# Which partitions of an expert's tile hold its tokens: a different order of the slots in every quarter

## The reference, cut to what matters

```
g_sel = argmax(t @ w_grp);  top_v, top_i = top_k(softmax(le_g), 2)
hid = einsum('nd,edf->nef', t, w_ein);  a, b = split(hid, 2)
act = silu(a) * b * combine[..., None]
out = einsum('nef,efd->nd', act, w_eout)
```

## Time and profile before

| | us |
|---|---|
| median of 3 runs | 752.68 (752.38 to 754.17) |
| profiled execution, its own time | 754.95 |
| span of the profiled execution | 753.3 |
| TensorE busy in the span | 697.9 (93%) |
| experts' stage, from the first sorted weights in flight to the last result row read | about 505 to 734 |

### The profile page before, as it was taken

One profiled execution on the slowest core, in us unless ns is written; L12 is line 12 of the kernel. 1 busy time (PEld: TensorE's weight loads), 2 busy tenths in 40 slices (PEclk: granted clock), 3 DMA queues, 4 the chain that ended last, 5 costly groups with the idle time before them and its releaser, 6 DMA issues.

```text
span 753.3 us, 12490 instructions
## 1 busy us (share of the span) xinstructions
PE 697.9 (93%) x4624; PEld 387.9 (51%) x4624; DVE 285.4 (38%) x898; ACT 171.9 (23%) x410; POOL 84.4 (11%) x127
## 2 busy tenths in 40 slices
PE   5899999999999999889999999999999997777894
PEld 2656666558765665544566666665333322222332
DVE  1553333621101787765451322484411211111257
ACT  0214444212101554332233001321110101110102
POOL 0301000001500334110000000001212121112000
PEclk9999999999999999999999999999999999999998
DMA  8999996727335883899999993538999999999981
GB/s 242 385 387 436 372 379 223 306 88 276 113 113 222 314 302 112 305 322 392 392 367 387 415 423 141 199 100 296 419 415 420 418 417 419 420 419 418 420 272 72
DMA packets 63269, 236.09 MB, mean 313 GB/s; under 512 B 9732, under 2 KB 20877, under 8 KB 48292
## 3 DMA queue, kind: packets, MB, share of 16 engines
q1 hardware_dynamic: 52884, 218.73, 74.7%
q0 software_dynamic: 6432, 14.74, 5.4%
q10 hardware_dynamic: 3888, 1.77, 0.9%
HBM read 230.52 MB, written 19.14 MB: 331 GB/s over the span
## 4 chain that ended last, share of the span: by engine, by line
PE 69%; SPq 13%; DMA 9%; DVE 3%; issue 3%; ACTq 1%; ACT 1%; POOL 0%; POOLq 0%; DVEq 0%
PE bank L637 14%; SPq L486 7%; PE bank L1189 6%; PE bank L1041 5%; PE bank L1068 5%; SPq L505 4%; DMA arena<-in_w_eout 4%; PE bank L1216 3%; PE bank L687 3%; PE bank L565 3%; PE bank L767 2%; PE bank L991 2%; PE bank L904 2%; DMA arena<-in_cmp_pages 2%; PE bank L866 2%
## 5 line engine op out<-in xcount | busy, mean ns | idle before, releaser
L1189 PE MATMUL bank<-arena 128*32 128x512 f32 (+1 forms) x896 | 107.6, 594 | 15.8 <-DMA arena<-in_w_ein 15.8
L637 PE MATMUL bank<-arena 128*128 128x320 f32 x384 | 106.6, 433 | 1.0 <-DVE arena L1596 1.0
L637 PEld LDWEIGHTS bank<-arena 128*128 128x128 f32 x384 | 71.5, 189 | 35.5 <-issue 6.4
L1189 PEld LDWEIGHTS bank<-arena 128*32 128x32 f32 (+1 forms) x896 | 30.6, 111 | 82.0 <-issue 73.7
L1216 PE MATMUL bank<-arena 128*32 128x512 f32 (+1 forms) x464 | 58.3, 595 | 6.6 <-DMA arena<-in_w_eout 6.2
L2076 DVE COPY arena<-bank 128x512 f32<-128x512 f32 x14 | 9.7, 692 | 105.8 <-PE bank L1147 105.8
L1518 ACT ACTIVATE arena<-bank 128x256 f32<-128x256 f32 x16 | 6.2, 386 | 148.6 <-PE bank L1189 145.3
L1041 PE MATMUL bank<-arena 128*128 128x320 f32 (+2 forms) x144 | 35.6, 408 | 0.0
L1216 PEld LDWEIGHTS bank<-arena 128*32 128x32 f32 (+1 forms) x464 | 15.6, 112 | 38.5 <-issue 30.0
L1342 ACT ACTIVATE arena<-bank 32x320 f32<-32x320 f32 x60 | 25.8, 430 | 41.7 <-PE bank L637 41.1
L1068 PE MATMUL bank<-arena 128*128 128x320 f32 x128 | 35.0, 432 | 0.0
(11 more groups left out here) (416 smaller groups left out, 1028.8 us busy)
## 6 DMA issues: line engine op xcount, KB each, us to landing
arena<-in_w_ein SPq DMA_DIRECT2D x52, 1024.0 KB, 25.4
arena<-in_w_eout SPq DMA_DIRECT2D x26, 1024.0 KB, 26.7
arena<-in_w_ada SPq DMA_DIRECT2D x12, 2048.0 KB, 12.4
arena<-in_w_in SPq DMA_DIRECT2D x10, 2048.0 KB, 9.0
arena<-in_k_pages SPq DMA_DIRECT2D x64, 320.0 KB, 6.3
arena<-in_v_pages SPq DMA_DIRECT2D x64, 320.0 KB, 9.5
arena<-in_w_ein SPq DMA_DIRECT2D x3, 4096.0 KB, 22.4
arena<-in_w_eout SPq DMA_DIRECT2D x3, 2048.0 KB, 16.3
```

Of the source, the lines that this page charges most:

```text
L637: m = mm(banks[c % 4][:, 0:N], ring[q][:, k, P * (c % 4):P * (c % 4 + 1)], hT[:, k, :], start=(k == 0), stop=(k == KD - 1))
L1189: m = mm(banks[2 + p % 2][r:r + n, :], xeT[p % 2][:, k, r:r + n], wi2[p % 3][:, e, k, :], start=(k == 0), stop=(k == KD - 1))
```

## The change

The constants alone change. In every quarter, the last eight partitions (24 to 31) now hold slots 4, 9, 14, 19, 24, 27, 29 and 31; the other 24 slots, in order, go to partitions 0, 8, 16, 1, 9, 17, 2, 10, 18, and so on up to 23. No instruction, DMA, wait or byte count is added or removed; the same number of slots is filled, in other partitions.

```diff
-    c[:, C_PLACE:C_PLACE + P] = (r // 32 * 32 + r % 4 * 8 + r % 32 // 4)[None, :]
+    place = r // 32 * 32 + r % 4 * 8 + r % 32 // 4
+    late = (4, 9, 14, 19, 24, 27, 29, 31)
+    others = [n for n in range(32) if n not in late]
+    for block in (0, 1, 2, 3):
+        for n, slot in enumerate(others):
+            place[32 * block + n % 3 * 8 + n // 3] = 32 * block + slot
+        place[32 * block + 24:32 * block + 32] = [32 * block + slot for slot in late]
+    c[:, C_PLACE:C_PLACE + P] = place[None, :]
```

## The result

The changed kernel takes 756.86 us, median of 7 runs (755.18 to 758.04), beside 753.01 for the kernel before (7 runs, 752.38 to 754.17): ratio 1.0043, 95% interval 1.0027 to 1.006, that is 2.0 to 4.5 us slower, 3.2 by the ratio itself and 3.85 between the two medians. Timed again later, beside parts of the change, it gave 1.0036 (1.0018 to 1.0053). The forecast was 755.9, 3.2 slower.

A forecast was written before the change was run, and what follows sets the result against it. The most loaded DMA engine was taken to end the experts' stage; 26 more rows at 0.146 us give 3.8, instruction packets allow 1.6, so 3.2 us slower, 755.9 us. Range 753.3 to 757.3.

The forecast's parts named there:

- Rival 1: Experts' stage: one engine's lateness doesn't matter, the stream has one rate; same time, 752.7 us; chance 0.09.
- Four neighbours of quarters 0 and 1, or 2 and 3, share an engine: Gathers and scatters: four neighbouring partitions of one quarter share a DMA engine with the same four of the next quarter.
- Rival 4: Experts' stage: eight neighbours share an engine; fullest 90 rows to 89, no change, 752.6 us; chance 0.04.
- The price of a filled slot, 0.146 us: Row queue: moving one token to another engine moves 0.157 - 0.011 = 0.146 us, an empty slot still having a tiny packet.
- rival 3: Row queue: a filled slot costs more, 0.185 or 0.2 us; 4.0 to 5.2 us slower, 756.7 to 757.9; chance 0.07.
- The fullest engine goes from 84 to 110 rows: 26 x 0.146 = 3.8 us: Gathers 3 to 15, scatters 0 to 13: added rows on the fullest engine delay the stage's end by 3.8 us, upper bound.
- The doubt about the instruction packets: Stage's end: instruction packets, 1.1 us each, up to two, may make another engine last before; cost down to 1.6 us.
- The figure of 3.2 us: Whole kernel: loss chosen in the upper half of the bounds 1.6 and 3.8 us, as three of the five fullest engines gain.
- Rival 2: Experts' stage: instruction packets sit on engines that lose rows; +1.6 us or less, 753.3 to 754.3; chance 0.11.
- Rival 5: Experts' stage: slow engines with each half's last partitions set the end and lose 20 rows; 2.9 us faster, 749.8; chance 0.03.
- The signs named for the profile: Next profile: last output weights near 729, DMA share falling earlier and deeper, TensorE's waits about 3 us more, scatter 4 0.3 later.
- The last scatter "0.3 later": Scatter 13 on the ending chain: up to 2 more rows, 0.3 us, covered by the last weights and already in the sum.

The follow-up runs named there:

- e1: The changed layout with the eight groups of four partitions of quarters 1 and 3 turned on by one group; ratio to the kernel before 1.0015 (0.9998 to 1.0031).
- e9: Kernel before with a table of places giving engine 8 alone 110 rows, the other fifteen even loads; ratio to before 1.002 (0.9994 to 1.0045).
- e11: Kernel before with a table of places giving engine 3 110 rows, engines 8 to 15 73 to 74; ratio to before 1.0057 (1.0035 to 1.0079).
- e2: Kernel before with slot n of a quarter in partition n, 136 rows on the fullest engine; ratio to before 1.0084 (1.0066 to 1.0103).
- e6: The change made in quarters 0 and 1 only, quarters 2 and 3 as in the kernel before; ratio to before 1.0028 (1.0006 to 1.005).
- e4: Kernel before with the order of the eight groups of four partitions reversed in all quarters; ratio to before 1.0017 (1.0001 to 1.0033).
- e7: Kernel before with the even table of places, worked out from this input's counts, nearly equal rows within each eight engines; ratio to before 0.9982 (0.9964 to 1.0001).
- e12: The even table of places timed again, unaltered, against the kernel before; ratio 0.9989 (0.9968 to 1.0011).
- e10: Kernel before with a table of places giving engine 8 136 rows, the other fifteen 63 to 65; ratio to before 1.0055 (1.0034 to 1.0077).
- e3: Kernel before with the order of the eight groups of four partitions reversed in quarters 1 and 3; ratio to before 1.0005 (0.9991 to 1.0019).

## Why the prediction was right, and where it was not

- **The stage ends with its most loaded engine, and not with the mean: right.** Same packets, same bytes, same dense stream, and the last landing moves between 193.1 and 200.4 us with the layout alone. Rival 1 falls.
- **Four neighbours of quarters 0 and 1, or 2 and 3, share an engine: right.** e1 differs from the change only in which groups of four meet on an engine. Quarters 0 with 2 would leave it as uneven as the change (109 rows each), and 0 with 3 does not fit e9 to e11. Rival 4 falls. The scatters' landings, from which I took it, are thin evidence: in e2 pairs 3 to 7 have 8 rows each on their fullest engine, and their scatters land after 8.2 to 9.8 us, pair 8 with 7 rows after 8.0.
- **The price of a filled slot, 0.146 us: right,** within a tenth (0.146 by the end of the span, 0.16 by the landing, 0.162 - 0.009 by the packets). The 0.185 and 0.2 of rival 3 are too high.
- **"The fullest engine goes from 84 to 110 rows: 26 x 0.146 = 3.8 us": the sum was right, the engine was not.** Engine 8 had 1.8 us of room and accounts for 2.0 of the 3.8 (e9). Engines 0 to 7 carry the same rows in e6 as in the change, and cost 1.8 there. Of the rest only 10, 12 and 14 gain rows. Engine 12 has 74 rows in the even table, one more than before, and that lands 1.0 earlier, so it had over 1.1 of room and 23 x 0.146 - 1.1 = 2.3 is the most it can cost; engine 14 gains 15 rows, 2.2. That leaves engine 10, with 79 to 104 rows: 25 x 0.146 = 3.65, beside 3.8 and 4.0 measured. So the last engine before was, or was level with, one of those of which the prediction said that it "gains rows too", with 3.4 to 3.7. This is worked out by elimination, and takes it that an engine keeps its room from one layout to the next; no row of a view names an engine.
- **The doubt about the instruction packets: the right size.** The two rooms measured, 1.8 us at 84 rows and 3.3 at 62, mean that apart from rows engine 3 is (84 - 62) x 0.146 - (3.3 - 1.8) = 1.7 us later than engine 8; the prediction allowed two packets of 1.1. That these packets make the rooms is still an argument: no run moved one. So what makes one engine later than another apart from its rows stays open.
- **The figure of 3.2 us: a hit, in part by luck.** It was a compromise between 1.6 and 3.8, made for the doubt about which engine is last. That doubt took nothing off: the last weights came the whole 3.8 later, the upper bound. The end is only 3.1 later because the last scatter, issued 3.5 later, took 0.8 less, where the prediction had up to 0.3 more, and the read took 0.4 more.
- **Rival 2** (the last engine before loses rows, 1.6 or less) falls: the time is 2.0 to 4.5 us longer and the last weights 3.8. **Rival 5** falls with the result, and with e4. The Trainium skill ("DMA: Bandwidth & Descriptors", section "Latency and other measured facts") calls engines 7 and 15 usually slower than the others; with 80 and 84 rows on them (e4) the last weights landed 194.2 us after the first scatter, as before, so this case's traces do not show them behind those that set the end. The Trainium skill's section "The descriptor swizzle" on that page gives this grouping of partitions for a plain transfer of 1 MiB; e1 and e9 to e11 bear it out for the indirect DMAs here.
- **The signs named for the profile.** Last output weights near 729: 728.5. DMA share lower and earlier: 0.72, 0.69, 0.49. Scatter 4 later by 0.3: 0.2, 8.2 against 8.0. TensorE's waits up by 3 us: wrong, they grew by 1.7, from 15.8 + 6.2 to these (us, times, longest):

```profile
PE bank L1189 <- DMA arena<-in_w_ein: 16.6, 11, 3.4
PE bank L1216 <- DMA arena<-in_w_eout: 7.1, 7, 1.6
```

  The other part is in the clock: from 600 to 690 the mean granted clock was 0.98 (1.00 before), so some of the same work took longer, by an estimate 0.02 of 71.69 = 1.4 us, and that much less waiting was left. The two profiles of the even table bear this out: 15.6 + 5.8 us of waits at 1.00 (e7), 14.4 + 5.3 at 0.98 (e12), with last weights 0.2 apart or less. So does e11, whose last weights are 3.7 late at 1.00: 15.9 + 8.8, 2.7 more than before. The weights set the pace either way.
- **The last scatter "0.3 later": wrong.** It took 0.84 less (7.93 against 8.77). While it is in flight the DMA share is 0.74 with the change, both times, and 0.59 in e2, and it takes 7.8 to 7.9 us; in the kernel before and eight others with it on the chain the share is 0.90 to 1.02 and it takes 8.55 to 8.97. In e10 it is not on the chain, and there too the share is 0.68 and it takes 7.84. It seems to land sooner where some engines have already run out of weights, and that outweighs two more rows; no run varied it alone.

## What to carry to other kernels

Where a stream keeps all 16 DMA engines busy and every transfer waits for its slowest engine, count the extra work per engine over the whole stretch: the fullest engine sets the cost, not the mean, and an uneven tile is harmless if the others load other engines (e1). Find first which partitions share an engine; spreading slots over the wrong groups, here eight neighbours instead of four, piles them up. And the engine with the most rows need not be the one that ends last: load one engine alone to measure its room.

## What the runs showed of the hardware that was not expected

- The engines are not alike apart from their rows: with 110 rows on engine 8 the last weights land after 196.2 us, with 110 on engine 3 after 197.9, and with the even table just four engines end 1.3 to 1.8 us behind all others.
- The stage begins at different times from one profile to the next: the first scatter lies between 528.7 (e9) and 533.0 (e3), for which I have no cause. It is not the table's doing as far as the times can tell, for they side mostly with the count from the first scatter and not with the span: e9, e6 and e11 have spans 1.7 and 0.2 shorter and 1.3 longer than before, from the first scatter they are 1.3, 2.2 and 4.0 longer, and by the ratios 1.5, 2.1 and 4.3.
- TensorE's granted clock fell inside the stage in some profiles. With the change it was 0.83 from 670 to 680, so part of the stretch at the lower of its two levels (1.2 instead of 2.4 GHz), after a stretch in which TensorE had been busy 6.01 of 10 us; before, after 6.68 of 10, it stayed at 1.00 (stretches of 10 us, after and before):

```profile
660.00:670.00 10.00, 6.01 (x54) 1.53 (x46) 1.08 (x2) 0.69 (x1) 2.02 (x2) 1.00 1.01 419
670.00:680.00 10.00, 9.63 (x72) 3.19 (x72) 1.02 (x2) 1.67 (x3) 0.00 (x0) 0.83 1.02 420
```

```profile
660.00:670.00 10.00, 6.68 (x62) 1.89 (x58) 1.08 (x2) 0.56 (x1) 2.02 (x2) 1.00 1.02 422
```

  Other profiles do not line up with this: in e3 it stayed at 1.00 after 6.05 of 10, in e1 it fell to 0.84 from 640 to 650 after 7.50. So what makes it fall is not shown. It did not set the time: e12, among the fastest, had 0.86 from 660 to 670.
